# Output projection, feed-forward norm and first query slot in two halves of the tokens

## The reference, cut to what matters

```
for l in range(2):
    sh1, sc1, g1, sh2, sc2, g2 = split(silu(c) @ w_ada[l] + b_ada[l])
    h = rmsnorm(x, norm_mix_g[l]) * (1 + sc1) + sh1
    y = mix_even(h) if l == 0 else mix_odd(h)
    x = x + g1 * y                                     # residual
    h = rmsnorm(x, norm_ffn_g[l]) * (1 + sc2) + sh2    # feed-forward norm
    x = x + g2 * peer(h)
# mix_odd: bg, cg, xt = split(h @ w_in)
#          y = (bg * causal_conv_w3(cg * xt)) @ w_out
# mix_even: conv branch (with a layer norm) and pooling branch, concatenated, @ w_out
# peer: q = h @ wq (16 blocks of 128); scores of each block against 128 keys; top 16;
#       gates g; sum over experts of g * gelu(u . h) * v
```

## Time and profile before

| what | value |
|---|---|
| median of 3 runs | 3735.47 us (3731.57 to 3738.09) |
| profiled execution | 3734.99 us |
| its span, first to last instruction | 3733.2 us |
| PE busy | 3621.0 us, 97% |
| DVE busy | 2594.7 us, 70% |
| ACT busy | 1014.6 us, 27% |
| mean granted PE clock | 0.986 of full speed |
| moved by DMA | 667.22 MB, mean 179 GB/s |

### The profile page before, as it was taken

How to read it: one execution, slowest core, us unless ns; L and a number is a source line. 1 busy time by engine, 2 the same in 40 slices (tenths; PEclk the granted TensorE clock), 3 DMA queues, 4 the chain that set the end, 5 groups by cost and what they waited for, 6 DMA issues and landing times.

```text
span 3733.2 us, 72787 instructions
## 1 busy us (share of the span) xinstructions
PE 3621.0 (97%) x31816; PEld 2962.5 (79%) x31816; DVE 2594.7 (70%) x3962; ACT 1014.6 (27%) x898; POOL 11.9 (0%) x34
## 2 busy tenths in 40 slices
PE   7879999999999999999989899999999999999998
PEld 3358888888888888888845688888888888888887
DVE  4967755566655888888845585565666488888886
ACT  3133333333342111111132333243333411111111
POOL 0000000000000000000000000000000000000000
PEclk9889999999999999999999999999999999999999
DMA  8921345464657455445322214364554764454541
GB/s 332 371 108 46 127 161 183 166 213 161 206 183 309 192 195 198 185 188 206 126 85 75 103 69 161 139 229 150 197 193 161 263 276 191 185 196 186 201 193 36
DMA packets 196231, 667.22 MB, mean 179 GB/s; under 512 B 11952, under 2 KB 151360, under 8 KB 152512
## 3 DMA queue, kind: packets, MB, share of 16 engines
q1 hardware_dynamic: 190608, 663.67, 47.7%
q10 hardware_dynamic: 5392, 0.56, 0.1%
q0 software_dynamic: 32, 0.01, 0.0%
HBM read 514.72 MB, written 149.49 MB: 178 GB/s over the span
## 4 chain that ended last, share of the span: by engine, by line
PE 93%; DVE 3%; DMA 2%; ACT 0%; issue 0%; SPq 0%; DVEq 0%; ACTq 0%
PE PS L757 38%; PE PS L707 37%; PE PS L682 5%; PE PS L601 4%; PE PS L737 3%; PE PS L581 2%; PE PS L646 1%; DMA arena<-whole_w 1%; DMA ring<-whole_w 1%; PE PS L695 1%; PE PS L623 1%; PE PS L596 1%; DVE H L1200 0%; DMA arena<-gates_dram 0%; DVE ring L1218 0%
## 5 line engine op out<-in xcount | busy, mean ns | idle before, releaser
L707 PE MATMUL PS<-X,ring 128*128 128x272 f16 x12288 | 1437.0, 279 | 0.0
L757 PE MATMUL PS<-arena,ring 128*128 128x272 f16 x12288 | 1424.1, 279 | 2.3 <-DVE ring L1218 1.2
L757 PEld LDWEIGHTS PS<-arena,ring 128*128 128x128 f16 x12288 | 1202.0, 98 | 224.3 <-issue 2.9
L707 PEld LDWEIGHTS PS<-X,ring 128*128 128x128 f16 x12288 | 1198.8, 98 | 218.7 <-issue 0.4
L1218 DVE SCALAR_TENSOR_TENSOR ring<-ring 128x4096 f16<-128x4096 f32 x149 | 659.1, 4423 | 608.8 <-ACT ring L895 600.2
L895 ACT ACTIVATE ring<-ring 128x4096 f16<-128x4096 f32 x149 | 538.6, 3615 | 1173.0 <-PE PS L757 1137.7
L1562 DVE TENSOR_TENSOR ACC<-PS,ACC 128x544 f32<-128x544 f32 x512 | 362.7, 719 | 232.1 <-PE PS L757 232.1
L1057 ACT ACTIVATE H<-PS 128x544 f32<-128x544 f32 x256 | 159.9, 625 | 974.4 <-PE PS L707 974.3
L1552 DVE TENSOR_TENSOR arena<-arena 128x544 f32<-128x544 f32 x256 | 292.1, 1141 | 45.1 <-DMA arena<-act_dram 45.1
L682 PE MATMUL PS<-X,ring 128*128 128x272 f16 x1536 | 188.4, 284 | 35.0 <-DVE X L1227 34.9
L682 PEld LDWEIGHTS PS<-X,ring 128*128 128x128 f16 x1536 | 149.7, 99 | 71.4 <-issue 41.0
(11 more groups left out here) (151 smaller groups left out, 1533.2 us busy)
## 6 DMA issues: line engine op xcount, KB each, us to landing
ring<-U SPq DMA_DIRECT2D x64, 2048.0 KB, 10.4
ring<-V SPq DMA_DIRECT2D x64, 2048.0 KB, 7.8
act_dram<-H SPq DMA_DIRECT2D x64, 1088.0 KB, 5.0
gates_dram<-ACC SPq DMA_DIRECT2D x68, 1024.0 KB, 5.6
arena<-gates_dram SPq DMA_DIRECT2D x32, 2176.0 KB, 9.4
arena<-act_dram SPq DMA_DIRECT2D x64, 1088.0 KB, 5.0
ring<-split_w SPq DMA_DIRECT2D x17, 2048.0 KB, 8.6
arena<-whole_w SPq DMA_DIRECT2D x11, 2048.0 KB, 11.3
```

Source lines behind the costliest of these rows:

```text
L707: mm = pe.matmul(ps_halves(u)[:, half, :], parts[lane][:, pu, k * 512 + j * P:k * 512 + (j + 1) * P], H16[:, ph, k, half * HALF:(half + 1) ...
L757: mm = pe.matmul(ps_halves(u)[:, half, :], parts[lane][:, pv, j * D + c * P:j * D + (c + 1) * P], WT[:, grp, pw, j, half * HALF:(half + 1) ...
```

## The change

- The output projection works on pairs of chunks and one half of the tokens (272 columns) at a time: pairs 0 to 3 for half 0, then pair 0 of half 1, the sums of squares of half 0, and pairs 1 to 3 of half 1 (`second_half`). A pair fills the two banks of one PSUM pair, one chunk in each; the number of matmuls is the same, but neighbours no longer alternate between the banks.
- Residual, squares, root, scaling, modulation and splitting are done for each half by itself, in 272 columns (half 1 in 240 and 32 where the conditioning matters). `X` is stored in two halves of 1,088-byte rows, and `H16` is laid out so that each half lies on its own half of `X`.
- The first query slot (chunks 0 to 3) runs as pairs and halves: pair 0 of half 0, the sums of half 1, pair 1 of half 0, pairs 0 and 1 of half 1. Scores 0 and 1 follow, then chunk c with the scores of c - 2.
- In layer 0, DVE's low part of the second output slot moves ahead of the root of the convolution's norm, since pairs 2 and 3 now begin there.
- In layer 1 the input slots come in the order Cg, xt, Bg. DVE multiplies Bg straight from PSUM; ACT's copy of it is gone.

The diff, cut to its core ("..." marks what is left out):

```diff
+ODD_ORDER = (2, 3, 4, 5, 0, 1)
...
+def _query_phase():
+    query, score, n = {}, {}, 4
+    for c in range(4):
+        query[c] = 2 + c // 2
+    for c in range(2):
+        score[c] = n + c
+    n += 2
+    for c in range(4, NQ):
+        query[c], score[c - 2] = n, n + 1
+        n += 2
+    score[NQ - 2], score[NQ - 1] = n, n + 1
+    return query, score
+QUERY_AT, SCORE_AT = _query_phase()
...
+        COLS = (slice(0, HALF), slice(HALF, T))
+        HALF_SEG = (((0, HALF, 0),), ((HALF, NP_, 0), (NP_, T, 1)))
...
-                            src = split_w[7 + i]
+                            src = split_w[7 + ODD_ORDER[i]]
...
-                sp.wait_ge(dve_read, RESIDUAL[l])
-                sp.dma_start(x_dram, X[:, :, :].rearrange("p k t -> p (k t)")).then_inc(x_stored, 16)
+                for h in range(2):
+                    sp.wait_ge(dve_read, RESIDUAL[l][h])
+                    sp.dma_start(x_dram.rearrange("p (k t) -> p k t", k=KD)[:, :, COLS[h]], X[:, :, COLS[h]]).then_inc(x_stored, 16)
...
+            def project(u, i, h, ks, start, stop, ready=None):
 
                 for k in ks:
                     if ready is not None:
                         ready(k)
-                    for n, (pw, ph) in enumerate(PASSES):
-                        for half in range(2):
-                            mm = pe.matmul(ps_halves(u)[:, half, :], parts[lane][:, pw, k * 512 + m * P:k * 512 + (m + 1) * P],
-                                           Z16[:, ph, k, half * HALF:(half + 1) * HALF],
+                    for c in range(2):
+                        at = k * 512 + (2 * i + c) % 4 * P
+                        for n, (pw, ph) in enumerate(PASSES):
+                            mm = pe.matmul(ps_halves(u)[:, c, :], parts[i // 2][:, pw, at:at + P], Z16[:, ph, k, COLS[h]],
                                            start=(start and n == 0 and k == ks[0]), stop=(stop and n == 2 and k == ks[-1]))
                 return mm
 
             def project_chunk(l, lane, c, ready=None):
 
...
+            def half_sums(l, h):
+                u = begin("dve")
+                for k in range(KD):
+                    if k % 2 == 0:
+                        pe.wait_ge(half_sq, 4 * (2 * l + h) + k // 2 + 1)
+                    mm = pe.matmul(ps_halves(u)[:, 0, :], ones[:, :], H[:, k, COLS[h]], start=(k == 0), stop=(k == KD - 1))
+                mm.then_inc(mm_done, 1)
+            def second_half(l):
+                for i in range(4):
+                    project(begin("dve"), i, 1, range(KD), True, True).then_inc(mm_done, 1)
+                    if i == 0:
+                        half_sums(l, 0)
...
+            def query_pair(l, i, h):
+                u = begin("act")
+                for k in range(KD):
+                    if i == 0:
+                        pe.wait_ge(h_split, (2 * l + h) * KD + k + 1)
+                    for c in range(2):
+                        at = k * 512 + (2 * i + c) * P
+                        for n, (pw, ph) in enumerate(PASSES):
+                            mm = pe.matmul(ps_halves(u)[:, c, :], parts[0][:, pw, at:at + P], H16[:, k, h, ph, :],
+                                           start=(k == n == 0), stop=(k == KD - 1 and n == 2))
+                mm.then_inc(mm_done, 1)
             def queries(l):
 
+                split_ready(0)
+                query_pair(l, 0, 0)
+                half_sums(l, 1)
+                query_pair(l, 1, 0)
+                query_pair(l, 0, 1)
+                query_pair(l, 1, 1)
                 pe.wait_ge(keys_in, 16 * (l + 1))
-                for c in range(NQ):
+                for c in range(2):
+                    scores(l, c)
...
-                    if c:
-                        scores(l, c - 1)
-                scores(l, NQ - 1)
+                    scores(l, c - 2)
+                for c in range(NQ - 2, NQ):
+                    scores(l, c)
...
+                    split_ready(1)
                     u2 = begin("dve")
-                    project(u2, 0, 2, range(KA, KD), True, False)
+                    project(u2, 2, 0, range(KA, KD), True, False)
                     u3 = begin("dve")
-                    project(u3, 0, 3, range(KA, KD), True, False)
-                    for m, u in enumerate((u0, u1, u2, u3)):
-                        project(u, 0, m, range(KA), False, True, lambda k: pe.wait_ge(z_ready, k + 1)).then_inc(mm_done, 1)
-                    split_ready(1)
-                    for m in range(2):
-                        project(begin("dve"), 1, m, range(KD), True, True).then_inc(mm_done, 1)
+                    project(u3, 3, 0, range(KA, KD), True, False)
+                    for i, u in enumerate((u0, u1, u2, u3)):
+                        project(u, i, 0, range(KA), False, True, lambda k: pe.wait_ge(z_ready, k + 1)).then_inc(mm_done, 1)
                 else:
-                    for c in range(4 * IN_SLOTS[1]):
...
+                    for i, slot in enumerate(ODD_ORDER):
+                        split_ready(i % 2)
+                        for c in range(4 * slot, 4 * slot + 4):
+                            project_chunk(1, i % 2, c, (lambda k: pe.wait_ge(hm_split, KD + k + 1)) if c == KD else None)
...
+            def square_pair(i, h):
+                w.take("dve")
+                act.wait_ge(dve_read, w.dve.at())
+                act.activation(H[:, 2 * i:2 * i + 2, COLS[h]], X[:, 2 * i:2 * i + 2, COLS[h]], ACT.Square).then_inc(half_sq, 1)
+            def modulate_half(l, h):
+                w.take("dve")
+                act.wait_ge(dve_read, w.dve.at())
+                act.activation(stat[:, 2, COLS[h]], stat[:, 0, COLS[h]], ACT.Abs_reciprocal_sqrt).then_inc(half_root, 1)
+                sh = mod_at["sh2"] * KD
+                for k in range(KD):
+                    act.wait_ge(half_xn, (2 * l + h) * KD + k + 1)
+                    for a, b, s in HALF_SEG[h]:
+                        ins = act.activation(H[:, k, a:b], H[:, k, a:b], ACT.Identity,
+                                             scale=scale[:, l, 1, k, s:s + 1], bias=mod[:, l, sh + k, s:s + 1])
+                    ins.then_inc(half_mod, 1)
...
+                    for lane in range(2):
+                        w.take("dve", KD // 2)
+                        high(lane, U_SCALE)
...
+                        act.copy(Z16[:, 0, c, :], BG[:, c, :]).then_inc(z_high, 1)
...
+                for i in range(4):
+                    square_pair(i, 0)
+                square_pair(0, 1)
+                modulate_half(l, 0)
+                square_two = w.dve.n
+                w.take("dve")
+                high(0, U_SCALE)
+                act.wait_ge(dve_read, square_two + 1)
+                act.activation(H[:, 2:4, COLS[1]], X[:, 2:4, COLS[1]], ACT.Square).then_inc(half_sq, 1)
+                for i in range(2, 4):
+                    square_pair(i, 1)
                 high(1, U_SCALE)
-                root()
...
+                take_pair(0, 0)
+                modulate_half(l, 1)
+                take_pair(1, 0)
+                take_pair(0, 1)
+                take_pair(1, 1)
+                high(0, U_SCALE)
+                for c in range(2):
+                    take_scores(c)
...
+            def half_inverse_root(l, h):
+                t, u = COLS[h], next_use()
+                dve.tensor_scalar(stat[:, 0, t], ps_halves(u)[:, 0, :], 1.0 / D, EPS, ALU.mult, ALU.add).then_inc(dve_read, 1)
+                dve.wait_ge(half_root, 2 * l + h + 1)
+                link(dve.tensor_tensor(stat[:, 1, t], stat[:, 0, t], stat[:, 2, t], ALU.mult))
+                link(dve.tensor_tensor(stat[:, 1, t], stat[:, 1, t], stat[:, 2, t], ALU.mult))
+                link(dve.tensor_scalar(stat[:, 1, t], stat[:, 1, t], -0.5, 1.5, ALU.mult, ALU.add))
+                link(dve.tensor_tensor(stat[:, 2, t], stat[:, 1, t], stat[:, 2, t], ALU.mult))
+            def half_norm(l, h):
+                half_inverse_root(l, h)
+                t, made = COLS[h], (2 * l + h) * KD
                 for k in range(KD):
-                    v = ps_halves(next_use())
-                    pieces = ((v[:, 0, :], 0, HALF, 0), (v[:, 1, 0:NP_ - HALF], HALF, NP_, 0), (v[:, 1, NP_ - HALF:HALF], NP_, T, 1))
-                    for y, a, b, s in pieces:
-                        ins = dve.scalar_tensor_tensor(out=X[:, k, a:b], in0=y, scalar=mod[:, l, mod_at["g1"] * KD + k, s:s + 1],
+                    dve.tensor_tensor(H[:, k, t], X[:, k, t], stat[:, 2, t], ALU.mult).then_inc(half_xn, 1)
+                dve.wait_ge(x_stored, 16 * (2 * l + h + 1))
+                for k in range(KD):
+                    dve.wait_ge(half_mod, made + k + 1)
+                    dve.tensor_copy(H16[:, k, h, 0, :], H[:, k, t]).then_inc(h_high, 1)
+                    dve.wait_ge(h_high, made + k + 1)
+                    dve.tensor_tensor(H16[:, k, h, 1, :], H[:, k, t], H16[:, k, h, 0, :], ALU.subtract).then_inc(h_split, 1)
...
+            def residual_pair(l, i, h):
```

(43 more changed lines are left out.)

144 lines of the change are left out of this document (57 added, 87 removed).

## The result

The changed kernel took 3696.68 us (median of four runs, 3695.63 to 3697.12) beside 3736.78 us for the kernel before on the same chip (3731.57 to 3738.41): a ratio of 0.9895, 95% interval 0.9880 to 0.9911, 40.1 us less, where 37.5 was forecast. Its profiled execution took 3696.33 us with a span of 3694.5, 38.7 less than the span of before.

The account below looks back on a forecast made before the run. PE, busy 97% of 3733.2 us, was taken as the bound, so only its idle or slow time could be won. Removed 41.1 less added 3.6 gives net 37.5 us, hence 3698.0 us; range 3692 to 3710.

Parts of the forecast that it names:

- The gaps and slow chunks: First query matmuls behind the feed-forward norm: two PE gaps of 17.34 us and 3.0 us of slow chunks each, 40.7 us removed.
- Half-wide instructions by slope: Norm chain on 272 columns: costs taken from slopes between rows; root 2.7 us, scaling 2.9, splits 0.69 a row.
- rival A: Half chains too long for their cover, as half-wide instructions cost more than the slope: 3705.6 us, at most 3727; chance 0.12.
- Cover of half 0: First query pair of half 0: PE sees the low weight half at 26.2 against 26.1, a wait of 0.1 us.
- Half 1: First query pair of the second token half: PE waits 1.0 us for the first split in each layer.
- Layer 1's new order: Bg last removes the 0.4 us wait for Z; the second output slot's last low half is hidden with 1.3 us to spare.
- Chunk 8: Queries: searches start at B + 2.3 (B: start of chunk 4); the low half is in time by 0.4 us.
- Rival B: Searches become the bound: one begins 5.1 us later, chunk 8 waits 4.7 us in each layer, 3707.4 us; chance 0.08.
- Rival C: Matmuls of a pair return to the same bank and may wait to drain; a doubling gives 3831 us; chance 0.04.
- Rival D: No overlap: a late store of 1,088-byte rows keeps PSUM full and PE stops as before, about 3735 us; chance 0.04.
- layer 0's low half, 1.4 us later: Moved ahead of the convolution norm's root, it makes root, Z and PE 1.4 us later; bounds 0 and 4.4.
- each us late is a us of PE: At half 0's first query pair, once the cover is gone, every us of delay costs PE one us.

Follow-up runs that it names:

- e8: The kernel before with 140 matmuls of 128x272 put into each of the two 17.3 us gaps at the first query chunk: 3736.64 us beside 3737.09.
- e4: The changed kernel without the refinement of the reciprocal root (four VectorE passes) in the four half chains: 3694.18 us.
- e3: The changed kernel with five more linked VectorE passes over 272 columns in each of the four half chains, ahead of the first split: 3710.52 us.
- e7: The changed kernel with layer 0's low half cut in two, half 1's sums inside the first query pair, V phase's first low half before the weighings: 3694.26 us.
- e2: The kernel before with only the odd input projection's new order (Bg last, read straight from PSUM): 3736.02 us beside 3736.54.
- e6: The changed kernel with four more linked VectorE passes over 272 columns ahead of the first search of each layer's queries: 3700.47 us.
- e1: The changed kernel with the odd input projection back in its old order (Bg first, copied from PSUM by ScalarE): 3698.80 us.
- e10: The kernel of e3 with 16 and 23 float32 matmuls put ahead of its two waits at the first query pairs in each layer: 3714.73 us.
- e5: The changed kernel with DVE's low half of layer 0's second output slot put back behind Z's chunks: 3710.24 us.
- e9: The kernel of e7 with 58 matmuls of 240 columns put where TensorE waits for Z in layer 0: 3693.50 us.

## Why the prediction was right, step by step

- **The gaps and slow chunks** (40.7 us): right, and e8 shows that the slow chunk was DVE's pace and not the clock: with the clock at 1.00 the stage is as long as before.
- **Half-wide instructions by slope**: right. Root stage 239.48 - 236.78 = 2.70 (2.7), scaling 2.90 (2.9), splits 0.69 a row. One instruction of 272 columns takes 0.44 us, but eight in a row come every 0.36 (2.90 for eight), so rival A is out. The Trainium skill's page "VectorE: DVE Perf Modes", section on the TRN2 errata, has a formula by which each takes an estimated 0.44 us; the trace agrees for one by itself and not for a row of them.
- **Cover of half 0** (t + 26.0 against 26.1, a wait of 0.1): low half at t + 26.0, and a wait of some 0.16 us by e4. e3 shows that the cover is as thin as said. **Half 1** (1.0): 0.99 in both layers; e4 and e7 take it away.
- **Layer 1's new order** (0.4 gained, margin 1.3): 0.7 gained (e2); the low half ends 9.6 us after the input, where 9.8 was said. **Store of a half**: 5.2 us, below the 7.5 taken.
- **Chunk 8** (searches B + 2.3, margin 0.4): B + 2.23, margin some 0.5; e6 turns 1.9 us more into a wait of 1.27 each. Rival B didn't come. **U group 1** (E + 20.8): E + 20.57.
- **Rival C**: 144 matmuls of pairs in 16.84 us, 117 ns each as before; returning to a bank costs nothing. **Rival D**: the store and the overlap are as forecast.
- **The term that was mis-sized: layer 0's low half, 1.4 us later.** Z came 0.5 us earlier in the first trace. The low half does push the root there (4.41 us behind the copy, 3.17 before, so 1.24), but the whole stage ahead ended 1.7 us sooner. Where the clock fell within the 16 sums, as in e6 (granted clock 0.56, against 1.00 in the changed kernel), they took 6.2 instead of 4.5 us; in e1, e3, e6 and e10 the root waited 0.37 us for them behind the low half, and there it costs nothing: the root stands 4.86 us behind the copy with the low half (e1) and without it (e5). That term is 0 to 1.2 us, by the clock of the run, beside a spread of 4 us in where that stage ends, which the working left out.
- **How near the total came** is in part luck. Z 0.5 us earlier instead of 1.4 later is 1.9 in favour; 0.45 were lost behind E, and the two layers' stages gave 38.6 instead of the 38.9 worked out: 37.5 becomes the span's 38.7. The medians' 40.1 is 1.4 more, since the profiled execution of before lies 1.8 us below its median of four and that of the changed kernel 0.35 below its own.
- **The step that was wrong, though it decided nothing here**: "each us late is a us of PE". By e3, waits of 2.38 and 3.37 us cost 1.5 to 1.7 us more each for the clock; waits of 0.99 (the changed kernel) and 1.27 us (e6) cost no such surplus. So where rivals A and B forecast waits of 2 us and more, their prices were too low; no run had rival B's wait of 4.7 us.

## What to carry to other kernels

A serial chain behind a reduction (sums, root, scale, split) is hidden by cutting the tokens in two when each half's chain, with every weight conversion in the same queue, is shorter than the other half's matmuls; work both out by slope and offset per instruction. Then look for what the earlier start collides with: here every margin was within 1.5 us, and the steps that protect them (order of the slots, the moved low half) are worth 1.7 and 10.9 us (e1, e5). Where a wait can't be removed and TensorE is the bound behind it, cheap matmuls into unused PSUM columns that end before the wait does keep its clock up (e9, 2.1 us); too long a filler gives most of it back (e10), and where another engine sets the pace behind the wait it gives nothing (e8).

## What the runs showed of the hardware

- TensorE waits of 0.99 us (query pairs) and 1.65 us (start of layer 0's V phase) in the changed kernel left the granted clock at 1.00. Waits of 2.38 and 3.37 us (e3) were followed by 0.50, the 1.2 GHz level, and by 1.5 to 1.7 us of lost time each on top of the wait. Behind a wait of 3.04 us in another stage (e10) the clock was 0.75 for 3 us and 0.68 for the next 3.
- A wait of 6.6 to 6.9 us cost 1.5 to 2.8 us behind it (18.4 to 19.6 us for what takes 16.84), differently in traces of the same instructions: 19.62 in the first trace of the changed kernel, 18.44 in the second. With TensorE busy through most of that wait (e9) it took 16.85.
- Each 128x128 float32 matmul stands in the trace as two records of 0.117 us, 0.23 us a matmul (3.73 us for 16).
